# Expert weights in 16 KB runs: twelve 1 MB transfers an expert become six of 2 MB

## The reference

```python
logits = xt @ w_router + b_router              # 264 x 32
top_v, top_e = lax.top_k(logits, 4)            # each token goes to 4 of 32 experts
gate_w = softmax(top_v)
# for each expert e, over the rows xb of its tokens:
gu  = xb @ w_gate_up[e] + b_gate_up[e]         # 1024 -> 2048
g, u = split(gu); g = minimum(g, 7); u = clip(u, -7, 7)
hid = (u + 1) * g * sigmoid(1.702 * g)
out = hid @ w_down[e] + b_down[e]              # 1024 -> 1024
# y[token] = sum over its experts of gate_w * out, then a layer norm
```

## Time and profile before

| | us |
|---|---|
| median of 3 runs | 1323.13 (1321.71 to 1324.47) |
| the profiled execution | 1330.0 |
| its span | 1328.3 |
| PE busy in the span | 1026.0 (77%) |
| DVE busy | 558.8 (42%) |
| POOL busy | 326.0 (25%) |
| ACT busy | 229.0 (17%) |
| moved by DMA | 499.13 MB, 376 GB/s on average |

### The profile page before, as it was taken

The page is one execution under the profiler, slowest core; times in us unless marked ns, Lnnn a source line. Parts: engine busy times, 40 slices in busy tenths (PEclk is TensorE's granted clock), DMA queues, the critical chain, the costliest instruction groups (busy, mean ns, idle before and its releaser), DMA issues.

```text
span 1328.3 us, 20414 instructions
## 1 busy us (share of the span) xinstructions
PE 1026.0 (77%) x7278; PEld 399.1 (30%) x7279; DVE 558.8 (42%) x952; ACT 229.0 (17%) x504; POOL 326.0 (25%) x228
## 2 busy tenths in 40 slices
PE   7997678986995899855466559966779975958956
PEld 5775343433331233211012113221212321222313
DVE  1699775438441445521112114522415451234414
ACT  1212352222211111200000101100111110101112
POOL 2576731204611110112221111111112102221110
PEclk9999588987997999977777769977989997889979
DMA  9986889898999949699999999899999989999992
GB/s 362 398 316 248 340 331 330 356 370 338 396 422 422 422 185 363 274 422 421 422 422 422 422 422 422 324 411 422 421 422 422 386 343 423 421 422 422 422 422 100
DMA packets 72404, 499.13 MB, mean 376 GB/s; under 512 B 7357, under 2 KB 7930, under 8 KB 19034
## 3 DMA queue, kind: packets, MB, share of 16 engines
q1 hardware_dynamic: 66336, 429.88, 79.1%
q0 software_dynamic: 4688, 67.26, 12.7%
q10 hardware_dynamic: 1354, 1.65, 0.3%
HBM read 496.06 MB, written 2.71 MB: 375 GB/s over the span
## 4 chain that ended last, share of the span: by engine, by line
DMA 41%; PE 36%; DVE 8%; POOL 6%; issue 5%; SPq 3%; ACT 1%; POOLq 0%; ACTq 0%; DVEq 0%
DMA pages_a<-in_w_gate_up 28%; PE bank L943 12%; PE bank L992 10%; DMA down_w<-in_w_down 7%; POOL gate_up_w L1521 3%; DMA gate_up_w<-in_w_gate_up 2%; DVE down_w L1583 2%; PE bank L727 2%; PE bank L816 2%; SPq L530 1%; PE bank L1004 1%; DMA pages_b<-in_cache_k,page_row 1%; PE bank L969 1%; PE bank L599 1%; DMA pages_b<-in_cache_v,page_row 1%
## 5 line engine op out<-in xcount | busy, mean ns | idle before, releaser
L943 PE MATMUL bank<-gate_up_w,pages_b 128*32 128x512 f32 x3264 | 446.5, 655 | 214.5 <-POOL gate_up_w L1521 208.4
L1521 POOL COPY gate_up_w<-pages_a 128x2048 f32<-128x2048 f32 x90 | 171.4, 1910 | 763.4 <-DMA pages_a<-in_w_gate_up 632.2
L1927 DVE TENSOR_TENSOR pages_b<-bank,work 32x512 f32<-32x512 f32 x100 | 68.4, 684 | 471.2 <-ACT work L1290 469.5
L943 PEld LDWEIGHTS bank<-gate_up_w,pages_b 128*32 128x32 f32 x3264 | 90.1, 114 | 456.2 <-POOL gate_up_w L1521 283.1
L992 PE MATMUL bank<-down_w,pages_b 128*32 128x512 f32 x1632 | 188.3, 594 | 12.2 <-DMA down_w<-in_w_down 12.2
L1290 ACT ACTIVATE work<-bank 32x512 f32<-32x512 f32 x100 | 58.8, 588 | 225.5 <-PE bank L992 224.3
L992 PEld LDWEIGHTS bank<-down_w,pages_b 128*32 128x32 f32 x1632 | 50.7, 110 | 145.6 <-issue 115.1
L1284 ACT ACTIVATE pages_b<-bank 128x256 f32<-128x256 f32 x51 | 19.5, 383 | 376.5 <-PE bank L969 376.5
L1952 DVE TENSOR_SCALAR pages_b<-bank 128x256 f32<-128x256 f32 x51 | 21.6, 424 | 143.4 <-PE bank L943 143.4
L599 PE MATMUL bank<-x_cols,gate_up_w 128*128 128x264 f32 x256 | 61.0, 400 | 0.6 <-ACT x_cols L1128 0.6
L599 PEld LDWEIGHTS bank<-x_cols,gate_up_w 128*128 128x128 f32 x256 | 49.9, 197 | 13.1 <-issue 2.3
(11 more groups left out here) (370 smaller groups left out, 1060.8 us busy)
## 6 DMA issues: line engine op xcount, KB each, us to landing
gate_up_w<-in_w_gate_up SPq DMA_DIRECT2D x166, 1024.0 KB, 15.3
down_w<-in_w_down SPq DMA_DIRECT2D x128, 1024.0 KB, 10.8
pages_a<-in_w_gate_up SPq DMA_DIRECT2D x90, 1024.0 KB, 16.3
gate_up_w<-in_w_in SPq DMA_DIRECT2D x4, 2048.0 KB, 18.8
gate_up_w<-in_w_out SPq DMA_DIRECT2D x1, 4096.0 KB, 18.3
pages_a<-in_w_in SPq DMA_DIRECT2D x1, 2048.0 KB, 25.8
pages_a<-in_w_mem_kv SPq DMA_DIRECT2D x1, 2048.0 KB, 27.7
down_w<-in_cache_mem_v SPq DMA_DIRECT2D x1, 2048.0 KB, 16.7
```

The costliest lines, as they stand in the source:

```text
L943: last = pe.matmul(p_gu[side][g * SLOTS:(g + 1) * SLOTS, :], xg_t[:, k % 4, k // 4, side * SLOTS:(side + 1) * SLOTS], gate_up_w[:, k, :].r ...
L1521: pool.tensor_copy(gate_up_w[:, k, :], staged[:, k, :]).then_inc(gu_in[k], 16)
L1927: dve.tensor_tensor(quad_rows[block * SLOTS:(block + 1) * SLOTS, h * HALF:(h + 1) * HALF], bank[1][h * PAIR:h * PAIR + SLOTS, :], down_par ...
```

## The change

All expert weights from expert 1 on move in pairs of tiles, as transfers of 2 MB with 16 KB a partition in one run. For gate/up the pair j holds rows j x 256 + 2p and j x 256 + 2p + 1 on partition p, so that a partition's two tiles are neighbours in the source. For down the array is laid out anew before the program starts (`down_pairs`), so that the four rows of a partition's two tiles are neighbours. The gathered rows are turned by every second column to match. Expert 0, in the front part, still comes tile by tile.

The semaphores of landings are per pair, so PE waits once for two tiles; SP waits for the use of both tiles of a pair before it issues the next one. The staged buffer holds one pair instead of three tiles: STAGED is 2. POOL still copies tile by tile, and each copy raises the pair's semaphore by half. The next pair is staged when both copies are done.

```diff
-    STAGED = 3
+    STAGED = 2
...
-            gu_k = w_gate_up[0].rearrange("e (k p) n -> e p k n", p=PARTS)
-            dn_k = w_down[0].rearrange("e (k p r) n -> e p k (r n)", p=PARTS, r=2)
+            gu_k = w_gate_up[0].rearrange("e (j p r) n -> e p j (r n)", p=PARTS, r=2)
+            dn_k = w_down[0]
...
             def load_expert(e, first):
...
-                for k in range(first, KC):
-                    sp.wait_ge(gu_used, last * KC + (k + 1))
-                    sp.dma_start(gate_up_w[:, k, :],
-                                 gu_k[bass.ds(e, 1), :, k, :].rearrange("a p n -> (a p) n")).then_inc(gu_in[k], 16)
-                for k in range(DK):
-                    sp.wait_ge(dn_used, last * DK + (k + 1))
-                    sp.dma_start(down_tiles[:, k, :],
-                                 dn_k[bass.ds(e, 1), :, k, :].rearrange("a p n -> (a p) n")).then_inc(dn_in[k], 16)
+                for j in range(first, KC // 2):
+                    sp.wait_ge(gu_used, last * KC + (2 * j + 2))
+                    sp.dma_start(gate_up_w[:, 2 * j:2 * j + 2, :].rearrange("p r n -> p (r n)"),
+                                 gu_k[bass.ds(e, 1), :, j, :].rearrange("a p n -> (a p) n")).then_inc(gu_in[j], 16)
+                for j in range(DK // 2):
+                    sp.wait_ge(dn_used, last * DK + (2 * j + 2))
+                    sp.dma_start(down_tiles[:, 2 * j:2 * j + 2, :].rearrange("p k n -> p (k n)"),
+                                 dn_k[bass.ds(e, 1), j, :, :].rearrange("a p n -> (a p) n")).then_inc(dn_in[j], 16)
...
             with sp.Fori(2, E) as e:
-                for k in range(STAGED):
-                    sp.wait_ge(gu_in[k], e * 16)
-                    sp.dma_start(staged[:, k, :],
-                                 gu_k[bass.ds(e, 1), :, k, :].rearrange("a p n -> (a p) n")).then_inc(stage_in[k], 16)
-                load_expert(e, STAGED)
+                sp.wait_ge(gu_in[0], e * 16 + 16)
+                sp.dma_start(staged.rearrange("p r n -> p (r n)"),
+                             gu_k[bass.ds(e, 1), :, 0, :].rearrange("a p n -> (a p) n")).then_inc(stage_in, 16)
+                load_expert(e, 1)
...
-                    last = pe.transpose(p_gather[:, j * PARTS:(j + 1) * PARTS], xg[:, j * PARTS:(j + 1) * PARTS], ident[:, :])
+                    last = pe.transpose(p_gather[:, j * PARTS:(j + 1) * PARTS],
+                                        xg.rearrange("p (j c r) -> p j r c", j=2, r=2)[:, j // 2, j % 2, :], ident[:, :])
...
-                pe.wait_ge(gu_in[k], e * 16 + 16)
+                if k % 2 == 0:
+                    pe.wait_ge(gu_in[k // 2], e * 16 + 32)
...
-                    pe.wait_ge(dn_in[k], e * 16 + 16)
+                    if k % 2 == 0:
+                        pe.wait_ge(dn_in[k // 2], e * 16 + 32)
...
+                pool.wait_ge(stage_in, e * 16 - 16)
                 for k in range(STAGED):
-                    pool.wait_ge(stage_in[k], e * 16 + (STAGE_IN - 16))
                     pool.wait_ge(gu_used, last * KC + (k + 1))
-                    pool.tensor_copy(gate_up_w[:, k, :], staged[:, k, :]).then_inc(gu_in[k], 16)
+                    pool.tensor_copy(gate_up_w[:, k, :], staged[:, k, :]).then_inc(gu_in[0], 8)
...
+def down_pairs(w):
+    layers, experts, rows, cols = w.shape
+    w = w.reshape(layers, experts, 2, 2, PARTS, 2, cols).transpose(0, 1, 2, 4, 3, 5, 6)
+    return w.reshape(layers, experts, 2, PARTS, 4 * cols)
```

More of the change, by code:

```diff
@@ L70, in layer_kernel @@
     E = w_router.shape[2]
-    FF = w_down.shape[2]
+    FF = b_gate_up.shape[2] // 2
     TOPK = 4
@@ L376, in layer_kernel @@
         ring_in = [[sem("ring_a_low_in"), sem("ring_a_high_in")], [sem("ring_b_low_in"), sem("ring_b_high_in")]]
-        gu_in = [sem(f"gate_up_in{k}") for k in range(KC)]
-        stage_in, STAGE_IN = (w_q_in, w_k_in, w_v_in)[0:STAGED], 16
-        dn_in = [sem(f"down_in{k}") for k in range(DK)]
+        gu_in = [sem(f"gate_up_in{k}") for k in range(KC // 2)]
+        stage_in = sem("staged_pair_in")
+        dn_in = [sem(f"down_in{k}") for k in range(DK // 2)]
         dve_n, pool_n = Counter(sem("dve_step")), Counter(sem("pool_step"))
@@ L492, in load_gate_up @@
                 for k in tiles_k:
-                    sp.dma_start(gate_up_w[:, k, :], gu_k[0, :, k, :]).then_inc(gu_in[k], 16)
+                    sp.dma_start(gate_up_w[:, k, :], gu_k[0, :, k // 2, k % 2 * 2 * FF:(k % 2 + 1) * 2 * FF])\
+                      .then_inc(gu_in[k // 2], 16)
             def load_down(*tiles_k):
                 for k in tiles_k:
-                    sp.dma_start(down_tiles[:, k, :], dn_k[0, :, k, :]).then_inc(dn_in[k], 16)
+                    sp.dma_start(down_tiles[:, k, :], dn_k[0, k // 2, :, k % 2 * 2 * D:(k % 2 + 1) * 2 * D])\
+                      .then_inc(dn_in[k // 2], 16)
             sp.wait_ge(mpv_done, 1)
@@ L2078 @@
     for name in _INS:
-        a = np.ascontiguousarray(inputs[name])
+        a = inputs[name]
+        if name == 'w_down':
+            a = down_pairs(np.asarray(a))
+        a = np.ascontiguousarray(a)
         arrays[f"in_{name}"] = a
```

## The result

The changed kernel takes 1336.7 us in the median of four runs (1334.0 to 1340.8), the kernel before 1322.5; the ratio is 1.0104, with a 95% interval of 1.0068 to 1.0141. Timed a second time beside other kernels it was 1335.9 us, ratio 1.0103 (1.0078 to 1.0129). So the change costs 9 to 19 us; the forecast was 1326 in a range from 1312 to 1342.

The account below looks back on a forecast made before the run. The expert stage was taken as bound by its weight transfer queue at 422 GB/s, with holes where releases come late. Terms -12 + 4 + 9 + 1 + 1 = +3 us gave 1326 us, range 1312 to 1342.

Parts of the forecast that it names:

- rivals of -9 and +19: Expert stage: faster transfers win, 1314 us, chance 25%; or down sent late in every expert, 1342 us, chance 15%.
- third rival: Weight transfers: longer runs gain nothing or only 0.6%, rate stays 422 to 425 GB/s; 1333 to 1338 us, chance 15%.
- Longer runs: Expert weight transfers: 16 KB runs move at 428 GB/s against 422, saving 12 us (0 to 21) over 27 experts.
- Fewer, larger waits: Start of each expert: PE waits for two serial copies, so the first down send comes later; 4 us lost (0 to 20).
- 10 us "by my sum": First down send: expected 10 us after the staged pair's landing, against 13 in the second rival.
- the limit: Latest first down send that keeps the queue fed: pair's landing plus three times 4.90, less 2.2 us lead.
- second rival: First down send: clock rises one tile later, some 20 experts lose 0.9 us each; +19, 1342 us, chance 15%.
- One megabyte less ahead: Pauses at long experts: SP stops after 2 MB instead of 3; 3.1 us at three places, +9 us (5 to 14).
- Ends: Stage start: second pair waits with 2 MB ahead, +1; stage end: one more tile behind the landing, +0.9 us.
- At nothing: Parts expected to cost nothing: fewer POOL copies, strided transposes of gathered rows (under 1 us), fewer DMA issues on SP.

Follow-up runs that it names:

- e3_short: Changed kernel with every 2 MB sent as two 1 MB transfers of 8 KB runs, counted by one semaphore; 1342.7 us, ratio 1.0145 to the kernel before.
- e5_both: Changed kernel with TensorE waiting for each staged copy by itself and down weights in four 1 MB transfers with own waits; 1320.4 us, ratio 0.9979 to before.
- e4_gates: Kernel before (1 MB transfers, three staged tiles) with only gate/up waits and releases made by pairs; 1331.0 us, ratio 1.0052.
- e1_split: Changed kernel with TensorE waiting for each of the two staged GpSimd copies by itself; 1332.8 us, ratio 1.0068 to the kernel before.

## Why the prediction came out as it did

- *The direction and the range held; the size did not.* +3 us was forecast, about +11 (traces) to +14 (medians) came. With a sum of +3 between rivals of -9 and +19 the direction was in good part luck: the chance put on slower was the largest, but 0.48. The time lies in the range, inside the third rival's 1333 to 1338, though not by its cause: the runs do gain.
- *Longer runs, -12 us.* Measured -14.3. The spacing is 428.6 GB/s, the 428 taken from the cache pages' queue. The rival in which they gain nothing is out: 1.6% was there (e3_short takes it back). The Trainium skill (DMA: Bandwidth & Descriptors, section on why small descriptors are slow) would give 0.6%, an estimate by its 3 cycles a packet; the trace does not agree, and the measurement decides.
- *Fewer, larger waits, +4 us: the step that failed.* Measured 12.3 in the first pair of traces, 8.4 in the second. The send itself was well placed: in the eight one-block experts whose pairs land between 570 and 790 it came 11.6 to 12.9 us after the landing, 12.3 in the mean, and two slow tiles make 12.1. The text's 10 us "by my sum" left the slow tiles out. PE's clock did not rise later: in these experts tiles 0 to 2 took 4.2 to 5.4 us, where two slow tiles and a fast one make 4.7 and three slow ones 5.8, and the granted clock of the window is 0.76 against 0.73. What failed is the limit, 12.5 us after the landing. It took the 2.2 us of lead of a 1 MB transfer for a 2 MB one, and it counted from the last completion alone. By 2.2 us the sends as they came in the first trace of the changed kernel would have lost 2.3 us. A 2 MB transfer into an empty queue lands after 7.6 us, 2.7 beyond its own 4.9; by 2.7 it would have been 7.9. It was 19.3: 16 of the 31 sends lost 0.6 us or more, where 0.2 each had been put down. Sends lost time up to about 4 us ahead of the last completion, and with 4 us the limit is 14.7 - 4 = 10.7 us after the landing; what makes the last stretch late, the distance between the engines or something else, stays open. e5_both shows that with the lead restored nothing is lost.
- *The second rival* (down late in every expert) had this place, but another cause: not a clock rising later, and 0.6 to 3.1 us lost in some 16 experts.
- *One megabyte less ahead, +9.* Gate/up lost 10.1 and 13.7 more in the two pairs of traces, the four pauses 15 more. The size is right, the places are not quite: each of the four pauses cost 3.0 to 4.2 more, also the first, which the prediction had left out because PE is the path there (18.2 to 22.3). e4_gates shows that the coarser release alone, with all three megabytes ahead, costs 7 to 9, which the prediction had at nothing. The two do not add up: tile 4 after the pauses lost 15.6 there, 10.0 and 7.7 before, and the pair 4 and 5 of the changed kernel 8.1 and 10.0. That the 4.9 us of the pair in flight cover the later release is a reading that fits.
- *Ends, +2.* The tail is 2.3 and 0.7 longer; one execution alone can't tell it from scatter (23.3 and 24.8 before). The 1.9 us ahead of the stage were in no term.
- *At nothing:* the strided transposes and the fewer issues left no mark; POOL copies fell from 171 us to 113, and nobody was waiting for the difference.

## What to carry to other kernels

Here longer transfers paid only by their rate; what they took is granularity, and it was paid where a landing or a release was waited for. Keep 1 MB pieces (and one wait per piece) where the consumer starts, or where a send follows a drained queue, and large ones where the queue is full anyway. Leave a send more lead than a lone transfer into an empty queue suggests: here that was 2.2 and 2.7 us, and sends were safe from 4.4 us ahead of the last completion. The distance between the engines seems to be part of the reason.

## What the runs showed of the hardware

- A queued 16 KB packet takes 611 ns, one of 8 KB 309 to 312: 1.6% in rate (421.9 to 428.6 GB/s).
- Into an empty queue a transfer needs its own time and 2.2 us more at 1 MB (4.7 us), 2.7 more at 2 MB. The changed kernel's direct gate/up transfers, as in the earlier trace rows; the shortest are those after a pause:

```profile
DMA to landing us min/median/max: 7.6/18.4/27.1
```

- The sixteen shares of a transfer stood 0.2 to 3.7 us apart, and in queued transfers they keep that distance until a late send or a pause (e1_split stood at 2.0 to 3.2 us from 606 to 821; the pause at 851 brought it to 0.7).
- At a late send most of the time goes to packets that take longer, not to engines without work. In e1_split the send at 613.01 came 3.5 us ahead of the last completion, 1.5 ahead of the first. From 614 on single packets took up to 1.85 us instead of 0.61, and the rate falls while the DMA share stays full (columns as in the earlier trace rows):

```profile
614.00:615.50 1.50, 1.50 (x18) 0.32 (x12) 0.28 (x1) 0.88 (x2) 0.00 (x0) 1.00 1.01 339
615.50:617.00 1.50, 1.50 (x18) 0.62 (x17) 1.08 (x2) 0.30 (x1) 0.00 (x0) 1.00 1.00 382
```

The distance between the engines grew there from 2.0 to 2.9 us. Around the late sends of the three traces in the table above the time of packets beyond 0.61 us makes 7.5 to 10.3 us a trace in the mean of the sixteen engines, that without a packet 3.4 to 4.8. In three late sends read packet by packet the slow packets begin within half a microsecond of the first engine's completion (e1_split at 614.1 and 644.9, the changed kernel at 648.2); why they are slow stays open.
